# 26 products that nothing reads, put into TensorE's queue at ten places of a two-block transformer kernel

## What is computed

```python
def hybrid_layer(x, w_in, ...):
    proj = x @ w_in                       # 1024 -> 3600 columns
    q, k, v = l2norm/silu(short_conv(proj...))
    ...
    kk = einsum("bhnid,bhnjd->bhnij", k_beta, kc)
    lower = eye + where(strict, kk * decay, 0)
    uw = triangular_solve(lower, rhs)     # per chunk and head
    ...
    _, o = lax.scan(step, s0, xs)         # the state goes from chunk to chunk
    ...
    y = concat([o_dn, o_gla]) @ w_out
    return layer_norm(ALPHA * x + y, ln_g, ln_b)
```

## Time and profile before

| | |
|---|---|
| device time, 3 runs | 2145.15 us median, 2144.42 to 2146.63 |
| profiled execution | span 2144.9 us from its first to its last instruction; the rest of its time is not shown |
| PE (TensorE matmul) busy | 2040.2 us, 95% |
| DVE (VectorE) / ACT (ScalarE) / POOL (GpSimd) busy | 1152.0 / 858.7 / 343.8 us |
| mean granted TensorE clock | 0.986 of full speed |

### The profile page before, as it was taken

How to read it: one execution, slowest core, us unless ns; L and a number is a source line. 1 busy time by engine, 2 the same in 40 slices (tenths; PEclk the granted TensorE clock), 3 DMA queues, 4 the chain that set the end, 5 groups by cost and what they waited for, 6 DMA issues and landing times. The chain is left out here.

```text
span 2144.9 us, 28160 instructions
## 1 busy us (share of the span) xinstructions
PE 2040.2 (95%) x11502; PEld 1608.1 (75%) x11502; DVE 1152.0 (54%) x1452; ACT 858.7 (40%) x1242; POOL 343.8 (16%) x310
## 2 busy tenths in 40 slices
PE   8999889899989889989899999999999999999998
PEld 5777886567788668744678888886889878888886
DVE  4445637554654753244458537735332957844763
ACT  4246424533642541255345324424113735423432
POOL 1200615030061530044130000022000012000002
PEclk9999999999999999999999999999999999999999
DMA  5211103222110322210222232232322012223221
GB/s 225 79 59 40 42 2 118 88 70 78 41 41 2 118 68 101 77 59 1 79 79 99 81 106 98 80 107 96 126 93 79 2 56 82 92 95 118 92 88 67
DMA packets 30564, 167.48 MB, mean 78 GB/s; under 512 B 2827, under 2 KB 9411, under 8 KB 14692
## 3 DMA queue, kind: packets, MB, share of 16 engines
q1 hardware_dynamic: 30004, 164.90, 22.2%
q10 hardware_dynamic: 432, 0.79, 0.1%
HBM read 159.35 MB, written 10.00 MB: 79 GB/s over the span
## 5 line engine op out<-in xcount | busy, mean ns | idle before, releaser
L301 PE MATMUL psum<-inputs_high,weights_high 128*128 128x512 f32 x928 | 383.2, 413 | 22.5 <-DVE inputs_low L249 14.8
L302 PE MATMUL psum<-inputs_low,weights_high 128*128 128x512 f32 x928 | 367.6, 396 | 0.0
L303 PE MATMUL psum<-inputs_high,weights_low 128*128 128x512 f32 x928 | 367.5, 396 | 0.0
L2073 PE MATMUL psum<-inputs_high,weights_high 128*128 128x512 f32 x704 | 276.1, 392 | 0.5 <-DVE inputs_low L2217 0.5
L2075 PE MATMUL psum<-inputs_high,weights_low 128*128 128x512 f32 x704 | 274.1, 389 | 0.0
L2074 PE MATMUL psum<-inputs_low,weights_high 128*128 128x512 f32 x704 | 274.0, 389 | 0.0
L254 DVE TENSOR_TENSOR weights_low<-weights_raw,weights_high 128x2048 fp32r<-128x2048 f32 x68 | 159.8, 2351 | 176.7 <-ACT weights_high L243 176.7
L301 PEld LDWEIGHTS psum<-inputs_high,weights_high 128*128 128x128 f32 x928 | 176.3, 190 | 80.7 <-DVE inputs_low L249 17.8
L302 PEld LDWEIGHTS psum<-inputs_low,weights_high 128*128 128x128 f32 x928 | 176.6, 190 | 41.1 <-issue 4.8
L243 ACT CAST weights_high<-weights_raw 128x2048 fp32r<-128x2048 f32 x68 | 129.0, 1898 | 195.0 <-PE psum L303 179.9
L303 PEld LDWEIGHTS psum<-inputs_high,weights_low 128*128 128x128 f32 x928 | 176.2, 190 | 40.4
(11 more groups left out here) (376 smaller groups left out, 3252.5 us busy)
## 6 DMA issues: line engine op xcount, KB each, us to landing
weights_raw<-w_stream SPq DMA_DIRECT2D x116, 1024.0 KB, 4.8
weights_raw<-w_down SPq DMA_DIRECT2D x32, 704.0 KB, 4.0
residual_parked<-residual SPq DMA_DIRECT2D x2, 2048.0 KB, 9.9
residual_back<-residual_parked SPq DMA_DIRECT2D x2, 2048.0 KB, 7.7
residual<-x_t SPq DMA_DIRECT2D x2, 1024.0 KB, 7.7
bias_by_row<-bias_rows SPq DMA_DIRECT2D x2, 1024.0 KB
bias_by_row<-bias_rows SPq DMA_DIRECT2D x1, 1536.0 KB
out_t<-residual SPq DMA_DIRECT2D x5, 256.0 KB, 2.3
```

The source lines that it names most:

```text
L301: pe.matmul(out, hi, self.ahi[:, k], start=start and b == 0, stop=False)
L302: pe.matmul(out, hi, self.alo[:, k], start=False, stop=False)
L303: mm = pe.matmul(out, lo, self.ahi[:, k], start=False, stop=stop and b == blocks - 1)
L2073: pe.matmul(out, wh, hi, start=start, stop=False)
```

## The change

A function `idle_products` issues products of constants (ones by the first 512 columns of the table of constants, both plain float32) into a PSUM bank that no one reads in that stage. It is called at these places of TensorE's list: at the start of the second layer's projections (2), at the end of `delta_gates` (2), after each left(0, t) of the solve (1, so 4), at the end of `solve` (2), at the end of `norms_and_output` (3), and at the start of `stick_projections` (2). Three of the stages run in each of two layers besides `norms_and_output`, so that there are 2 + 2x(2 + 4 + 2 + 3) + 2 = 26 products. Nothing is taken away, and no wait is added or dropped.

```diff
+def idle_products(pe, k, bank, count):
+
+    for _ in range(count):
+        pe.matmul(k.ps[:, bank], k.con[:, K_ONES:K_ONES + P], k.con[:, 0:T], start=True, stop=True)
...
                 if layer == 0:
                     pe.wait_ge(k.first_params, 32)
                     small_rows(range(KD))
+                else:
+                    idle_products(pe, k, 7, 2)
                 behind = 3
...
                     if n in (1, 3):
                         turn(HEADS + 2 + n // 2)
+                idle_products(pe, k, 4, 2)
...
                 for t in range(TT):
                     left(0, t)
+                    idle_products(pe, k, 7, 1)
                 for m in range(first_step, steps + behind):
                     if m < steps:
                         left(m // TT, m % TT)
                     if m - behind >= first_step:
                         both((m - behind) // TT, (m - behind) % TT)
+                idle_products(pe, k, 7, 2)
...
                 pe.matmul(ps[:, 2], ones, before[:, KD - 1], start=False, stop=True).then_inc(s.squares, 1)
+                idle_products(pe, k, 7, 3)
...
                     elif last >= 0:
                         pe.wait_ge(s.freed, last + 1)
 
+                idle_products(pe, k, 7, 2)
                 behind = 3
```

## The result

The changed kernel took **2153.39 us** (median of 5 runs, 2151.11 to 2153.94), the kernel before 2145.15 us (5 runs beside it, 2144.42 to 2146.90). The medians differ by 8.2 us and the means by 7.3. The ratio is 1.0031 with a 95% interval of 1.002 to 1.0042: slower by 0.31%. Experiment 7 measures it again on another chip, 1.0047. The forecast was 2149.0 us; the measured time lies 4.4 us above it and 0.4 us above the upper end of its range.

What follows compares the result with a forecast made beforehand. Stages of small steps passed between engines, and stage ends where all engines meet, set the time. Terms +2.0 - 1.0 + 1.5 + 0.1 + 1.7 = +4.3 us on 2144.9 gave 2149.2, stated as 2149.0 us; range 2144.5 to 2153.0.

Steps and rivals of the forecast that it cites:

- the fourth rival: Both seams fall to half clock again and the solve's end keeps half clock: 2151 to 2155 us, chance 0.2.
- End of the gates: Two products before the solve, in both layers, delay the meeting of engines by 1.0 us each: +2.0 us.
- a Block's end doesn't wait for idle products: Rival: products at the gates and norms cost nothing, the solve's end only the scan's delay; 2140 to 2143 us, chance 0.07.
- Level 0: Products after the lefts of the solve's first level cost 0 and keep full clock, left(1, 3) 0.5 us sooner: -1.0 us.
- End of the solve: Two products before the scan cost +2.4 and +3.0 us; the scan's first chunk returns 1.5 and 2.35: net +1.5 us.
- No return: Upper bound at the solve's end, the scan's first chunk giving nothing back: +3.0 us in each layer.
- End of the norms: Three products, in both layers, end almost exactly with ScalarE's last instruction: +0.05 us each, +0.1 in all.
- The seams: Two products at each next stage's start are covered; full clock gains nothing, TensorE waits about 3.2 us for the third tile.
- The wait that takes its place: The 3.2 us wait at a seam may bring 3.4 us of half clock, costing 1.7; one such fall counted: +1.7 us.
- The mean clock: Sign: TensorE's mean clock rises from 0.986 to between 0.989 and 0.993 without the time falling.
- the forecast's own band: The forecast as it stands: 2147.5 to 2150.5 us, chance 0.35.
- The rule: Throttled time priced at half: the 41 us at the treated places would give back 20 us, time about 2125 us.

Runs made afterwards that it cites:

- Experiment 7: The changed kernel and the kernel before, both unaltered, measured once more on one other chip: ratio 1.0047.
- `seams_only`: Kernel before plus only the products at the ends of the norms and the starts of the next stages: 2150.11 us, ratio 1.0008.
- `all_again`: The changed kernel, unaltered, run and profiled again on another chip beside the kernel before: 2156.56 us, ratio 1.0047.
- `behind_meeting`: Changed kernel with one product at the start of solve and scan replacing two before each, level 0 kept, none at norms and seams: 2146.30 us, ratio 0.9999.
- `level0_only`: Changed kernel cut to one product behind each left of the solve's first level, all others removed: 2146.14 us, ratio 1.0001 against the kernel before.
- `solve_end_again`: Changed kernel cut to the two products at the end of the solve, profiled a second time on another chip: 2155.65 us (one run).
- `none_again`: The kernel before, unchanged, run for a second profile: 2149.41 us (one run).

## Why the prediction was right and wrong

The direction and the mechanisms held; the size was short, forecast +3.9 and measured +8.2 us by the medians here (+7.3 by the means) and +10.9 ± 1.5 by the means on another chip. Between the two first profiles the treated stages came to +3.8, close to the forecast's +4.3, but that is partly luck: the solve's end was 0.8 us dearer than forecast and the fall behind the seams 1.1 us cheaper. The other 3.0 us lie in stages for which the forecast had no term. The measured time falls into the band of the fourth rival (2151 to 2155), whose condition, that both seams fall, was not met in that profile.

- **End of the gates: right**, +1.9 for +2.0, in every trace that has the products, and shown by one product costing 0.11. With it falls the rival that a Block's end doesn't wait for idle products. A fixed price for each product falls too, since the second cost 0.85 us and the first 0.11.
- **Level 0: right in kind.** Full clock held, and left(1, 3) started at 253.33, 10.79 us after the meeting in place of 11.11. That is 0.3 us for the 0.5 expected: the level's later lefts had also to wait for ScalarE's copy (an idle 0.31 us before the left at 251.91, in the same timeline). Up to VectorE's last instruction the solves were shorter by 0.94 and 0.18 us, -1.1 for the -1.0 forecast; in layer 0 most of it came behind level 1, so that the sum fits by luck. Alone the part is worth -0.6 ± 1.0.
- **End of the solve: the term that was mis-sized.** I let the clock rise within layer 0's products (+2.4 there, +3.0 in layer 1) and took the whole give-back as sure, net +1.5. The products cost 3.2 us in both layers. In the first profile the scans gave back 1.68 and 2.5, net about +2.3; where half clock lasts into the scan they give back 0.16. Measured alone the part is +4.3 ± 1.6. "No return" was bounded at +3.0 each and weighed only in the fourth rival, together with two falls at the seams, at 0.2: one execution of the kernel before can't say how long the half clock lasts in another. The delay itself was 3.24 us for the 3.0 of two products at half clock.
- **End of the norms: right**, +0.04 each.
- **The seams: right that they don't pay.** The third tile is as late as before and TensorE waits 2.93 and 3.08 us (3.2 was said).
- **The wait that takes its place: right in kind, undersized in sum.** In the first profile one seam fell, for 0.62 us and not 1.7. Elsewhere the layer seam took 2.7 us (`seams_only`) and 4.2 (`all_again`): there the third tile's fall came, and a second stretch of 3.4 and 6.8 us followed some 60 us later in the same stage, which the prediction had no term for. That the seams' products cause these falls isn't shown: `behind_meeting`, without them, also has one, at 395.2, for 1.07 us, and `level0_only` and `solve_end_again`, also without them, fall at the stick seam.
- **The mean clock**, foretold at 0.989 to 0.993, came to 0.987: the end of the solves stayed at half, and new half clock stood at other places. Those that cost time lie in stages without a product and cost 3.0 of the 6.9 us between the two profiles. `none_again` has a like +1.79 in the first projections without any product, so that part isn't put down to the change. The +1.30 in the stick attention is less clear. It came in four profiles (the kernel after, `solve_end_again`, `level0_only` and `behind_meeting`), each with a fall behind the stick seam, but not in `all_again`, which has that fall too, and in neither profile of the kernel before.
- **A slip in the chances.** The borders put "slower" above 2149.4, and a little over half of the forecast's own band was counted there. With a point of 2149.0 and a band of 2147.5 to 2150.5, little over a third of it lies there.
- **The rule** of the Trainium skill, "TensorE: Matmul & The Clock Gate", part on the HAM clock gate, by which throttled time returns half, is not borne out for the kernel as a whole: its 20 us did not come. For the greater part that is because the half clock did not go. By the mean clocks it was some 60 us before and 56 after, reckoned as in the prediction. Where it did go, what came back depends on the place. At the layer seam and in the norms nothing came back (211.74 and 211.75 us; 66.14 and 66.18). In layer 0's solve something did: with full clock and no late product it took 39.83 us, with 8.3 us at half 43.22, and some 2 of these 3.4 us are left when the 1.3 that arose at full clock are taken off. By the rule of the Trainium skill an estimate would be half of 8.3, 4.1 us. The remark in the same part of the Trainium skill that a kernel's half-clock products vary from run to run agrees with the two traces of the kernel before.

Measured alone, the four parts come to +1.4 - 0.6 + 4.3 + 2.5, +7.5 us before rounding, each to ± 1 or more, and the whole to +7.3 by the means here and +10.9 ± 1.5 on another chip: they add up as well as these runs can tell. Why half clock falls on one execution's first projections and not on another's stays open.

## What to carry to other kernels

Work put in to keep the clock up costs nothing only where it ends before the thing that the engine waits for anyway: ahead of a meeting of all engines no more than the engine's lead (0.73 us here), in a chain of short steps none (a product of 256 columns cost 0.63 us a step). Half-clock time in front of a wait that another engine ends is worth nothing back; in a chain through TensorE it is worth something, but less than the products that would remove it cost here. Where the time depends on when the clock falls, one profile of each side holds some 3 us of accident, and only a dozen runs of each part told which one lost.

## What the runs showed of the hardware beyond that

- One and the same program spread over 13 us (2138.96 to 2152.14 in 69 runs), though its first five lay within 2.5 us of each other.
- Two gapless products of 3.78 us did not lift the clock, and 2.4 us of gapless products before them neither (the stretch of 278.50 to 292.20 in `solve_end_again`, 12.18 of its 13.70 us busy). In the kernel after, TensorE was busy for all 6.80 us from 76.80 to 83.60 and at half clock throughout.
- Waits of 2.9 to 3.1 us were followed by a fall at one seam and not at the other in the same execution (the kernel after).
